# Seven block products in place of eight for six of the 16 row tiles of each FFN gate/up pair

## The chip, the cores and the metric

One core of a Trainium2 chip runs the kernel. The metric is the device time of one execution in microseconds. Three executions of the kernel before are shown; their median is 2152.19 us.

## The reference

An encoder trunk of two layers over 256 tokens of width 2048, in float32. Layer 0 mixes with a Conformer convolution and a windowed attention side by side, layer 1 with a short gated convolution. Behind each stands a SwiGLU FFN with D_FF = 5632, and it is the FFNs that the change touches:

```python
def swiglu_ffn(h, w_gate, w_up, w_down):
    return (jax.nn.silu(h @ w_gate) * (h @ w_up)) @ w_down

# for each layer:
    x = x + mixer(rms_norm(x, mix_norm_g[layer]))
    h = rms_norm(x, ffn_norm_g[layer])
    x = x + swiglu_ffn(h, w_gate[layer], w_up[layer], w_down[layer])
```

## The kernel before

**Numbers and slots.** Every float32 operand is split in two parts, high (rounded to fp32r) and low (the rest), and a product is three matmuls into one PSUM bank: high × high, high × low, low × high (L510 to L512 in `slots`). Activations lie transposed in SBUF, as stationary operands of 128x128: `xT_hi`, `xT_lo` hold the normed input with 16 row tiles of the model width, each for two token halves (t = 0, 1). Weights stream. A slot is 2 row tiles of 512 columns, 512 KB: SP loads it into `w_raw`, ScalarE makes `w_hi` (L871), and the low part `w_lo` is made by VectorE for even slots (L1216) and by GpSimd for odd ones (L464). TensorE then runs 2 row tiles × 2 token halves × 3 = 12 matmuls of 512 columns on it. `w_raw`, `w_hi` and `w_lo` are rings of 4: ScalarE's high of slot s waits until TensorE has used slot s − 4, and SP's load of slot s until the low of slot s − 4 is made.

**Jobs and banks.** A job is a run of slots that ends in one pair of PSUM banks (`pair0`, `pair1`, `pair2`, one bank for each token half). The order of all work is written out by hand, each engine's queue on its own, with the numbers of slots as the common clock: "lows(a, b)" on VectorE stands for the low parts of the slots a to b − 1, "highs(a, b)" for ScalarE's.

**The FFN.** For each of the 11 column blocks of 512 of D_FF: a gate job (16 row tiles, 8 slots, pair 0), an up job (8 slots, pair 1). ScalarE reads the gate pair through SiLU, scaled by the norm's `rstd`, into `gated` (L925); VectorE multiplies the up pair by `rstd` and `gated` into `mixed` (L1271); TensorE transposes `mixed` in 8 small matmuls (L546) in the middle of the next gate job, ScalarE (L892) and VectorE (L1242) split the result into `yT_hi` and `yT_lo`. After all 11 blocks the down projection runs as four jobs, one for each 512 columns of the model width, with 22 slots each over all 44 row tiles of y; VectorE adds each pair into the residual `xs` (L1290, `add_pair`). The blocks 1 to 10 are a hardware loop on each engine; the down jobs are straight code.

**The first block of an FFN** shares its time with the end of the mixer: the last of four blocks of `xs` is transposed and split (`x_split`: L1230, L882, L1235), and the norm is formed (`norm_stats`, `norm_root`), since `rstd` is only needed where the first gate is read. TensorE's `first_block` waits for each x block just ahead of the slots that use it.

## Time and profile before

| | us |
|---|---|
| timed executions, median (lowest, highest) | 2152.19 (2150.77, 2154.49) |
| the profiled execution, from its first to its last instruction | 2149.2 |
| busy: TensorE matmuls, VectorE, ScalarE, GpSimd | 2109.6, 828.8, 994.1, 981.8 |
| GpSimd's low parts (L464), 370 of them | 899.4 |
| VectorE's low parts (L1216), 370 of them | 514.8 |
| ScalarE's high parts (L871), 740 of them | 782.0 |

The page gives no other time of the profiled execution than its span; the median of the timed ones is 3.0 us above that. A matmul's duration in a row (0.39 us) is longer than the distance to the next, since matmuls overlap in the array: their pace is read from the starts. A row of a group gives the smallest, the middle and the largest duration.

### The profile page before, as it was taken

The page shows a single profiled execution, that of the slowest core. Times are in us where ns is not written, and L with a number is a line of the kernel's source. Part 1 is how long each engine was busy: PE and PEld are TensorE (multiplying, and loading weights), DVE is VectorE, ACT ScalarE, POOL GpSimd, SP SyncE. Part 2 cuts the span into 40 slices and gives each one's busy share as a digit, 9 for nine tenths or more (in the row PEclk, how much of TensorE's full clock was granted, in tenths as well). Part 3 has the DMA queues.
Part 4 walks back from the last instruction along what each step waited for, and adds up shares of the span by engine and source line. Part 5 has one row for each costly group of instructions (what it writes and reads, how often), then busy time and mean ns, then how long its engine had stood idle before and what let it go on. Part 6 is the DMA issues. An engine that isn't in the chain of part 4 may idle for free.

```text
span 2149.2 us, 26716 instructions
## 1 busy us (share of the span) xinstructions
PE 2109.6 (98%) x9780; PEld 1757.2 (82%) x9780; DVE 828.8 (39%) x932; ACT 994.1 (46%) x1208; POOL 981.8 (46%) x471
## 2 busy tenths in 40 slices
PE   8999889999999999999999999999999999999999
PEld 6888678888888888888888888888888888888887
DVE  4786854323323322333243444442232232322221
ACT  6677555444444443444444444454444444443332
POOL 3676634444444444444344444444444444444443
PEclk9999999999999999999999999999999999999999
DMA  7543446666666665555566555566666666655554
GB/s 235 167 129 108 147 137 188 184 194 188 187 192 185 186 195 193 186 189 191 181 189 199 183 182 187 193 185 190 194 182 189 193 188 189 191 188 193 192 192 165
DMA packets 208930, 393.65 MB, mean 183 GB/s; under 512 B 12000, under 2 KB 22240, under 8 KB 208864
## 3 DMA queue, kind: packets, MB, share of 16 engines
q1 hardware_dynamic: 208576, 392.22, 58.3%
q8 instruction: 44, 0.72, 0.1%
q10 hardware_dynamic: 288, 0.53, 0.1%
q14 instruction: 22, 0.18, 0.0%
HBM read 390.60 MB, written 2.10 MB: 183 GB/s over the span
## 4 chain that ended last, share of the span: by engine, by line
PE 55%; issue 30%; POOL 9%; DVE 4%; ACT 2%; DMA 1%; POOLq 0%; DVEq 0%; SPq 0%; ACTq 0%
PE pair L510 18%; PE pair L512 18%; PE pair L511 18%; POOL w_lo L464 8%; PE tbank L546 1%; DVE pair L1319 1%; DVE w_lo L1216 1%; ACT w_hi L871 1%; POOL cv L477 1%; DMA w_raw<-in_w_in 1%; PE pair L530 0%; PE pair L531 0%; PE pair L532 0%; DVE xs L1290 0%; ACT products L960 0%
## 5 line engine op out<-in xcount | busy, mean ns | idle before, releaser
L464 POOL TENSOR_TENSOR w_lo<-w_raw,w_hi 128x1024 fp32r<-128x1024 f32 x370 | 899.4, 2431 | 1152.5 <-ACT w_hi L871 1152.5
L871 ACT ACTIVATE w_hi<-w_raw 128x1024 fp32r<-128x1024 f32 x740 | 782.0, 1060 | 932.6 <-PE pair L512 904.4
L1216 DVE TENSOR_TENSOR w_lo<-w_raw,w_hi 128x1024 fp32r<-128x1024 f32 x370 | 514.8, 1393 | 1203.0 <-ACT w_hi L871 1202.8
L510 PE MATMUL pair<-w_hi,xT_hi 128*128 128x512 f32 x1920 | 751.3, 391 | 1.8 <-DVE w_lo L1216 1.0
L512 PE MATMUL pair<-w_hi,xT_lo 128*128 128x512 f32 x1920 | 747.9, 390 | 0.0
L511 PE MATMUL pair<-w_lo,xT_hi 128*128 128x512 f32 x1920 | 747.8, 389 | 0.0
L510 PEld LDWEIGHTS pair<-w_hi,xT_hi 128*128 128x128 f32 x1920 | 360.8, 188 | 77.5 <-POOL w_lo L464 1.7
L512 PEld LDWEIGHTS pair<-w_hi,xT_lo 128*128 128x128 f32 x1920 | 360.7, 188 | 75.3
L511 PEld LDWEIGHTS pair<-w_lo,xT_hi 128*128 128x128 f32 x1920 | 361.0, 188 | 73.9
L510 PE MATMUL pair<-w_hi,yT_hi 128*128 128x512 f32 x704 | 274.3, 390 | 0.0
L512 PE MATMUL pair<-w_hi,yT_lo 128*128 128x512 f32 x704 | 273.9, 389 | 0.0
L511 PE MATMUL pair<-w_lo,yT_hi 128*128 128x512 f32 x704 | 273.9, 389 | 0.0
L512 PEld LDWEIGHTS pair<-w_hi,yT_lo 128*128 128x128 f32 x704 | 132.1, 188 | 27.5
L510 PEld LDWEIGHTS pair<-w_hi,yT_hi 128*128 128x128 f32 x704 | 132.1, 188 | 27.3
L511 PEld LDWEIGHTS pair<-w_lo,yT_hi 128*128 128x128 f32 x704 | 132.2, 188 | 27.2
L477 POOL TENSOR_TENSOR cv<-products,cv 128x256 f32<-128x256 f32 x96 | 83.4, 893 | 2.6
L510 PE MATMUL pair<-w_hi,mT_hi 128*128 128x512 f32 x128 | 52.4, 410 | 10.9 <-DVE mT_lo L1532 9.4
L1319 DVE SCALAR_TENSOR_TENSOR pair<-uT,cols,pair 128x256 f32<-128x256 f32 x139 | 59.2, 479 | 1.1
L925 ACT ACTIVATE gated<-pair,rstd 128x512 f32<-128x512 f32 x54 | 34.2, 686 | 40.6 <-PE pair L512 40.6
L511 PE MATMUL pair<-w_lo,mT_hi 128*128 128x512 f32 x128 | 51.0, 399 | 0.0
L512 PE MATMUL pair<-w_hi,mT_lo 128*128 128x512 f32 x128 | 50.9, 398 | 0.0
L510 PE MATMUL pair<-w_hi,zT_hi 128*128 128x512 f32 x128 | 50.2, 392 | 0.0
(132 smaller groups left out, 1116.4 us busy)
## 6 DMA issues: line engine op xcount, KB each, us to landing
w_raw<-in_w_gate SPq DMA_DIRECT2D x176, 512.0 KB, 4.3
w_raw<-in_w_up SPq DMA_DIRECT2D x176, 512.0 KB, 3.9
w_raw<-in_w_down SPq DMA_DIRECT2D x176, 512.0 KB, 4.2
w_raw<-in_sc_in SPq DMA_DIRECT2D x96, 512.0 KB, 4.4
w_raw<-in_w_in SPq DMA_DIRECT2D x52, 512.0 KB, 3.9
w_raw<-in_w_out SPq DMA_DIRECT2D x32, 512.0 KB, 3.7
w_raw<-in_sc_out SPq DMA_DIRECT2D x32, 512.0 KB, 4.3
xs<-in_x SPq DMA_DIRECT2D x4, 512.0 KB, 8.5
```

Source lines behind the costliest of these rows:

```text
L464: nc.gpsimd.tensor_tensor(w_lo[:, place, :, :], w_raw[:, place, :, :], w_hi[:, place, :, :].bitcast(F32), ALU.subtract).then_inc(w_lo_odd, 1)
L477: nc.gpsimd.tensor_tensor(cv[:, c, :], products[:, n % PRODUCTS, :], cv[:, c, :], ALU.add).then_inc(pool_tap_done, 1)
L510: nc.tensor.matmul(o, hi[:, k, tok(t)], w_hi[:, r, kk, :], start=first, stop=False)
L511: nc.tensor.matmul(o, hi[:, k, tok(t)], w_lo[:, r, kk, :], start=False, stop=False)
L512: mm = nc.tensor.matmul(o, lo[:, k, tok(t)], w_hi[:, r, kk, :], start=False, stop=end)
L546: mm = nc.tensor.transpose(tbank[b][:, n * P:(n + 1) * P], source, ident)
L871: nc.scalar.activation(w_hi[:, r, :, :], w_raw[:, r, :, :], ACT.Copy).then_inc(w_hi_ready, 1)
L925: ins = nc.scalar.activation(dest[:, t, :], pairs[pair][t][:, :], func, scale=rstd[:, t:t + 1])
L1216: nc.vector.tensor_tensor(w_lo[:, r, :, :], w_raw[:, r, :, :], w_hi[:, r, :, :].bitcast(F32), ALU.subtract).then_inc(w_lo_even, 1)
L1319: nc.vector.scalar_tensor_tensor(dest, u, w, acc, ALU.mult, ALU.add).then_inc(tap_done, 1)
```

## The change

**The unit.** Gate and up of one column block no longer are two jobs but one `unit`. Of the 16 row tiles, the tiles 0 to 2 and 4 to 6 are taken as the two blocks of a 2x2x2 block product: the two token halves are the block rows, the two groups of tiles the inner index, gate and up weights the block columns. The eight block products of it are replaced by seven, of sums and differences of activation blocks (`xS_hi`, `xS_lo`, and the place of tiles 0 to 2 of the second half in `xT`) and of weight blocks. VectorE overwrites the four loaded weight blocks (3 row tiles × 512 columns, 768 KB each, in `s_raw`) with differences in four steps (`remake`: place 0 twice, places 2 and 3 once). The other ten row tiles stay ordinary slots of two tiles (`REST_K`). A unit has 17 ring places ("ops"): seven products (ops 0, 1, 3, 5, 6, 9, 12) of 9 matmuls and ten slots of 12.

**Low parts.** In a unit GpSimd makes those of the ops 8, 11 and 14 (`POOL_PLACES`), VectorE all others, the products' too (128x1536). Outside the units they alternate as before.

**Sums.** Products that belong to more than one result are added by VectorE from pair 2 into `snap` in four steps of 512 columns (the first after a copy by ScalarE, `snapshot`), and `gate_sums` and `up_sums` (1024 columns each) add the banks of pair 0 and pair 1. SiLU reads `snap`, `multiply` forms `mixed` from `snap` and `gated`. Up is not scaled by `rstd` there; the down sum into `xs` is (`add_down`).

**Chunks.** SBUF does not hold y for all blocks beside `s_raw`, so the FFN runs in three chunks of 3, 4 and 4 units, each with its share of the down projection (four jobs over 12, 16 and 16 row tiles) and its four sums into `xs`. The last y block of a chunk is used at the end of the first two jobs (`("end", ...)`).

**Around it.** The x sums for the units are made where the blocks 0 and 1 of x are split (`sums_first`, `sums_second`), during the output projection of the mixer. All hardware loops become straight code. `bg` of the gated mixer loads its slots in plain order.

```diff
+SK = 3
+UNIT_OPS = 17
+POOL_PLACES = (8, 11, 14)
+PRODUCT_PLACES = {0: 0, 1: 1, 3: 0, 5: 3, 6: 0, 9: 2, 12: 3}
+MADE = {3: 1, 6: 2, 9: 3, 12: 4}
+REST_K = ((3, 7), (8, 9), (10, 11), (12, 13), (14, 15))
+CHUNKS = ((0, 3), (3, 7), (7, 11))
 RMS_EPS = 1e-6
 LN_EPS = 1e-5
...
+    def unit(self, name):
+        self.units[name] = (len(self.units), self.slots, list(self.pair_uses))
+        for i in range(UNIT_OPS):
+            self.operand(i not in PRODUCT_PLACES, i in POOL_PLACES)
+        self.pair_uses = [uses + 1 for uses in self.pair_uses]
...
+                for ch, (u0, u1) in enumerate(CHUNKS):
+                    for i in range(u0, u1):
+                        n, o, _ = UNIT[(layer, i)]
+                        if n:
+                            sp.wait_ge(t_made, 4 * n)
+                            low_done(sp, UNIT_BASE[n - 1] + 6)
+                        block(0, gates, 0, i)
+                        block(1, ups, 4, i)
+                        rest(o + 2, ups, 0, i)
+                        if n:
+                            low_done(sp, UNIT_BASE[n - 1] + 9)
+                        block(2, ups, 0, i)
+                        rest(o + 4, ups, 1, i)
+                        if n:
+                            low_done(sp, UNIT_BASE[n - 1] + 12)
+                        block(3, gates, 4, i)
+                        rest(o + 7, gates, 0, i)
+                        rest(o + 8, ups, 2, i)
+                        rest(o + 10, gates, 1, i)
+                        rest(o + 11, ups, 3, i)
+                        rest(o + 13, ups, 4, i)
+                        rest(o + 14, gates, 2, i)
+                        rest(o + 15, gates, 3, i)
+                        rest(o + 16, gates, 4, i)
...
+            def unit(layer, i, before=None, norm=None, last_out=None):
+                n, o, uses = UNIT[(layer, i)]
+                a, e = pairs[2][0][:, :], pairs[2][1][:, :]
+                b, a2 = pairs[0][0][:, :], pairs[0][1][:, :]
+                c = pairs[1][0][:, :]
+                if norm is not None:
+                    pe.wait_ge(lo_ready, LOW[("x", norm, 0, 0)] + 1)
+                pe.wait_ge(pair_read[2], uses[2])
+                product(o, a, xT_hi[:, 0:SK, tok(0)], xT_lo[:, 0:SK, tok(0)], True)
+                if norm is not None:
+                    pe.wait_ge(lo_ready, LOW[("s4", norm)] + 1)
+                pe.wait_ge(pair_read[1], uses[1])
+                product(o + 1, c, xS_hi[:, 2, :, :], xS_lo[:, 2, :, :], True, False)
+                rest(o + 2, 0, 1, (False, True))
+                if norm is not None:
+                    read_out(last_out)
+                    x_transposes(norm, NJ - 1)
+                product(o + 3, e, xT_hi[:, 0:SK, tok(1)], xT_lo[:, 0:SK, tok(1)], True)
+                if norm is not None:
+                    x_split(norm, 2)
+                rest(o + 4, 1, 1, (False, False))
+                if before is not None:
+                    y_transposes(layer, before)
+                pe.wait_ge(pair_read[0], uses[0])
+                product(o + 5, b, xT_hi[:, 4:4 + SK, tok(0)], xT_lo[:, 4:4 + SK, tok(0)], True, False)
+                pe.wait_ge(snapped, n + 1)
+                product(o + 6, a, xS_hi[:, 0, :, :], xS_lo[:, 0, :, :], True)
+                rest(o + 7, 0, 0, (False, True))
+                rest(o + 8, 2, 1, (False, False))
+                pe.wait_ge(u2_ready, n + 1)
+                product(o + 9, a, xS_hi[:, 1, :, :], xS_lo[:, 1, :, :], True)
+                rest(o + 10, 1, 0, (False, False))
+                if norm is not None:
+                    x_split(norm, 3)
+                rest(o + 11, 3, 1, (False, False))
+                product(o + 12, a2, xT_hi[:, 4:4 + SK, tok(1)], xT_lo[:, 4:4 + SK, tok(1)], False, False)
+                rest(o + 13, 4, 1, (False, False), (True, True))
+                rest(o + 14, 2, 0, (False, False))
+                rest(o + 15, 3, 0, (False, False))
+                rest(o + 16, 4, 0, (False, False), (True, True))
...
+            def silus(layer, i):
+                n, o, uses = UNIT[(layer, i)]
+                act.wait_ge(pair_read[0], uses[0] + 1)
+                if n:
+                    act.wait_ge(mixed_ready, n)
+                for t in range(TT):
+                    ins = nc.scalar.activation(gated[:, t, :], snap[:, t, :], ACT.Silu, scale=rstd[:, t:t + 1])
+                ins.then_inc(gated_ready, 1)
+            def snapshot(n, o):
+                act.wait_ge(w_used, o + 1)
+                if n:
+                    act.wait_ge(gated_ready, n)
+                nc.scalar.activation(snap[:, 0, :], pairs[2][0][:, :], ACT.Copy).then_inc(snapped, 1)
...
+            def unit(layer, i, at, before=None, norm=None):
+                n, o, _ = UNIT[(layer, i)]
+                highs(at, o + 4)
+                if before is not None:
+                    silus(layer, before)
+                snapshot(n, o)
+                highs(o + 4, o + 7)
+                if norm is not None:
+                    x_highs(norm, NJ - 1)
+                    x_squares(NJ - 1)
+                highs(o + 7, o + 8)
+                if before is not None:
+                    y_highs(layer, before)
+                highs(o + 8, o + 9)
+                if norm is not None:
+                    norm_root(norm)
+                highs(o + 9, o + 10)
+                highs(o + 10, o + 13)
+                highs(o + 13, o + 17)
+                if norm is not None:
+                    act.wait_ge(rstd_ready, norm + 1)
+                return o + 17
...
+            def remake(n, step, dest, a, b):
+                nc.vector.tensor_tensor(s_raw[:, dest, :, :], s_raw[:, a, :, :], s_raw[:, b, :, :],
+                                        ALU.subtract).then_inc(t_made, 1)
+            def bank_sum(dest, bank, source):
+                return nc.vector.tensor_tensor(dest, bank, source, ALU.add)
+            def gate_sums(layer, i):
+                n, o, uses = UNIT[(layer, i)]
+                dve.wait_ge(w_used, o + UNIT_OPS)
+                dve.wait_ge(u3_ready, n + 1)
+                bank_sum(snap[:, 0:2, :], banks[0][:, :, :], snap[:, 0:2, :]).then_inc(pair_read[0], 1)
+            def up_sums(layer, i):
+                n, o, uses = UNIT[(layer, i)]
+                dve.wait_ge(w_used, o + 14)
+                dve.wait_ge(pair_read[2], uses[2] + 1)
+                bank_sum(snap[:, 2:4, :], banks[1][:, :, :], snap[:, 2:4, :]).then_inc(pair_read[1], 1)
+            def multiply(layer, i):
+                n, o, uses = UNIT[(layer, i)]
+                dve.wait_ge(pair_read[1], uses[1] + 1)
+                dve.wait_ge(gated_ready, n + 1)
+                nc.vector.tensor_tensor(mixed[:, :, :], snap[:, 2:4, :], gated[:, :, :],
+                                        ALU.mult).then_inc(mixed_ready, 1)
+            def y_lows(layer, i):
+                k = BK * (i - [u0 for u0, u1 in CHUNKS if u0 <= i][-1])
+                for t in range(TT):
+                    low_of_group(("y", layer, i, t), yT_hi, yT_lo, slice(k, k + BK), t)
+            def unit(layer, i, at, before=None, after=None, norm=None):
+                n, o, uses = UNIT[(layer, i)]
+                lows(at, o + 2)
+                dve.wait_ge(s_loaded[2], 16 * (n + 1))
+                remake(n, 1, 0, 2, 0)
+                lows(o + 2, o + 3)
+                if before is not None:
+                    gate_sums(layer, before)
+                if after is not None:
+                    after()
+                lows(o + 3, o + 4)
+                if before is not None:
+                    multiply(layer, before)
+                else:
+                    lows(o + 4, o + 5)
+                dve.wait_ge(t_made, 4 * n + 1)
+                remake(n, 2, 0, 1, 0)
+                if before is not None:
+                    lows(o + 4, o + 5)
+                lows(o + 5, o + 7)
+                if norm is not None:
+                    x_split(norm, NJ - 1)
+                dve.wait_ge(t_made, 4 * n + 2)
+                remake(n, 3, 2, 1, 2)
+                lows(o + 7, o + 8)
+                if before is not None:
+                    y_lows(layer, before)
+                lows(o + 8, o + 9)
+                if norm is not None:
+                    norm_stats(norm)
+                lows(o + 9, o + 10)
+                remake(n, 4, 3, 3, 0)
+                dve.wait_ge(w_used, o + 7)
+                if n:
+                    dve.wait_ge(gated_ready, n)
+                bank_sum(snap[:, 1, :], pairs[2][0], snap[:, 0, :]).then_inc(u2_ready, 1)
+                lows(o + 10, o + 11)
+                dve.wait_ge(u2_ready, n + 1)
+                if n:
+                    dve.wait_ge(mixed_ready, n)
+                bank_sum(snap[:, 2, :], pairs[2][1], snap[:, 1, :]).then_inc(w_sum_ready, 1)
+                lows(o + 11, o + 13)
+                dve.wait_ge(w_used, o + 10)
+                dve.wait_ge(w_sum_ready, n + 1)
+                bank_sum(snap[:, 1, :], pairs[2][0], snap[:, 1, :]).then_inc(u3_ready, 1)
+                lows(o + 13, o + 14)
+                dve.wait_ge(u3_ready, n + 1)
+                bank_sum(snap[:, 3, :], pairs[2][1], snap[:, 1, :]).then_inc(pair_read[2], 1)
+                lows(o + 14, o + 17)
+                up_sums(layer, i)
+                return o + 17
...
```

## Rows read from the trace of the kernel before

**Rows 1.** Page: busy us (share of span) xinstructions; granted clock in 40 slices.

```profile
PE 2109.6 (98%) x9780; PEld 1757.2 (82%) x9780; DVE 828.8 (39%) x932; ACT 994.1 (46%) x1208; POOL 981.8 (46%) x471
...
PEclk9999999999999999999999999999999999999999
```

**Rows 2.** Waits, whole span: who waited for whom, us, times, longest.

```profile
ACT w_hi L871 <- PE pair L512: 904.4, 595, 2.6
...
PE pair L510 <- DVE mT_lo L1532: 9.4, 1, 9.4
```

**Rows 3.** Timeline, TensorE, in block 9 of FFN 0: start, us, engine, line.

```profile
734.48 0.39 PE L512 MATMUL pair<-w_hi,xT_lo 128*128 128x512 f32 x1
734.71 1.03 PE L546 MATMUL tbank<-tables,mixed 128*128 128x128 f32 x8
...
741.05 0.39 PE L510 MATMUL pair<-w_hi,xT_hi 128*128 128x512 f32 x1
```

**Rows 4.** Timeline, ScalarE, same stretch.

```profile
735.45 1.09 ACT L892 ACTIVATE yT_hi<-tbank 128x512 f32 x2 [2.20 <-PE tbank L546]
...
741.25 1.06 ACT L871 ACTIVATE w_hi<-w_raw 128x1024 fp32r<-128x1024 f32 x1 [1.66 <-PE pair L512]
743.97 1.06 ACT L871 ACTIVATE w_hi<-w_raw 128x1024 fp32r<-128x1024 f32 x1 [1.66 <-PE pair L512]
```

**Rows 5.** Timeline, VectorE, 640 to 800.

```profile
650.77 1.41 DVE L1216 TENSOR_TENSOR w_lo<-w_raw,w_hi 128x1024 fp32r<-128x1024 f32 x1 [2.12 <-ACT w_hi L871]
...
661.65 1.97 DVE L1216 TENSOR_TENSOR w_lo<-w_raw,w_hi 128x1024 fp32r<-128x1024 f32 x1 [4.21 <-ACT w_hi L871]
...
679.60 1.41 DVE L1271 SCALAR_TENSOR_TENSOR mixed<-pair,rstd,gated 128x512 f32<-128x512 f32 x2 [0.40 <-PE pair L512]
...
724.02 1.41 DVE L1271 SCALAR_TENSOR_TENSOR mixed<-pair,rstd,gated 128x512 f32<-128x512 f32 x2 [0.40 <-PE pair L512]
...
736.21 1.29 DVE L1242 TENSOR_TENSOR yT_lo<-tbank,yT_hi 128x512 f32 x2 [1.71 <-ACT yT_hi L892]
```

**Rows 6.** Timeline, TensorE: two stalls, in brackets.

```profile
274.87 0.79 PE L510 MATMUL pair<-w_hi,mT_hi 128*128 128x512 f32 x1 [9.44 <-DVE mT_lo L1532]
...
343.75 0.50 PE L510 MATMUL pair<-w_hi,xT_hi 128*128 128x512 f32 x1 [0.41 <-POOL w_lo L464]
```

**Rows 7.** Windows: us, busy of each engine (xinstructions), clock, DMA share, GB/s.

```profile
10.00:15.00 5.00, 3.68 (x12) 3.06 (x13) 4.26 (x7) 3.73 (x8) 1.54 (x1) 1.00 1.05 388
150.00:164.00 14.00, 12.70 (x97) 12.62 (x96) 9.73 (x13) 9.21 (x17) 10.74 (x10) 0.88 0.45 134
330.00:380.00 50.00, 49.59 (x226) 40.83 (x226) 20.77 (x21) 24.71 (x30) 22.89 (x9) 1.00 0.62 193
820.00:1060.00 240.00, 240.00 (x1077) 199.07 (x1076) 72.27 (x66) 100.60 (x107) 107.69 (x44) 1.00 0.58 190
```

**Rows 8.** Lines L1216, L1235, L1319: duration ns min/median/max, first and last start.

```profile
L1216 DVE TENSOR_TENSOR w_lo<-w_raw,w_hi x370: 1208/1226/3422, 9.3 to 2132.3; 128x1024 fp32r<-128x1024 f32 x185
...
L1235 DVE TENSOR_TENSOR xT_lo<-scaled,xT_hi x32: 679/690/950, 11.9 to 1429.1; 128x512 fp32r<-128x512 f32 x32
...
L1319 DVE SCALAR_TENSOR_TENSOR pair<-uT,cols,pair x139: 471/477/491, 73.3 to 254.3; 128x256 f32<-128x256 f32 x139
```

**Rows 9.** Timeline, GpSimd, 640 to 670.

```profile
648.70 2.40 POOL L464 TENSOR_TENSOR w_lo<-w_raw,w_hi 128x1024 fp32r<-128x1024 f32 x1 [4.56 <-ACT w_hi L871]
...
660.13 2.40 POOL L464 TENSOR_TENSOR w_lo<-w_raw,w_hi 128x1024 fp32r<-128x1024 f32 x1 [4.20 <-ACT w_hi L871]
```

**Rows 10.** Timeline, VectorE, at the first gate block of FFN 0.

```profile
334.77 1.29 DVE L1230 TENSOR_TENSOR scaled<-tbank,cols 128x512 f32<-128x512 f32 x2 [0.79 <-PE tbank L546]
...
340.90 0.16 DVE L1254 SCALAR_TENSOR_TENSOR rstd<-newton,root 128x2 f32<-128x2 f32 x1
```

**Rows 11.** Timeline, ScalarE, same stretch.

```profile
335.50 1.24 ACT L882 ACTIVATE xT_hi<-scaled 128x512 fp32r<-128x512 f32 x2 [2.77 <-DVE scaled L1230]
...
338.77 1.28 ACT L912 ACT_TABLE_LOAD   x1
```

More of the change, by code:

```diff
@@ L70, in job @@
         self.jobs[name] = (self.slots, pair, self.pair_uses[pair])
-        self.slots += k_tiles // slot_k
+        for _ in range(k_tiles // slot_k):
+            self.operand(True, self.slots % 2 == 1)
         self.pair_uses[pair] += 1
@@ new lines, in rest @@
+            def rest(o, q, pair, first, last=(False, False)):
+                r = o % RING
+                low_done(pe, o)
+                for kk in range(SLOT_K):
+                    k = REST_K[q][kk]
+                    for t in range(TT):
+                        b = pairs[pair][t][:, :]
+                        end = last[t] and kk == SLOT_K - 1
+                        nc.tensor.matmul(b, x_hi(k, t), w_hi[:, r, kk, :], start=(first[t] and kk == 0), stop=False)
+                        nc.tensor.matmul(b, x_hi(k, t), w_lo[:, r, kk, :], start=False, stop=False)
+                        mm = nc.tensor.matmul(b, x_lo(k, t), w_hi[:, r, kk, :], start=False, stop=end)
+                mm.then_inc(w_used, 1)
@@ L647, in _ @@
             narrow("kv", 2, SN)
-            slots("q0", 0, 6, xT_hi, xT_lo, last=SD)
+            slots("q0", 0, 6, x_hi, x_lo, last=SD)
             pe.wait_ge(qk_normed, 1)
@@ new lines, in ffn @@
+            def ffn(layer, norm, last_out, norm_after):
+                for ch, (u0, u1) in enumerate(CHUNKS):
+                    if ch == 0:
+                        unit(layer, 0, None, norm, last_out)
+                    else:
+                        unit(layer, u0)
+                    for i in range(u0 + 1, u1):
+                        unit(layer, i, i - 1)
+                    down(layer, ch, norm_after if u1 == NF else None)
+            ffn(0, 1, ("conv_out", NJ - 1), 2)
+            for b in range(2):
+                x_split(2, b)
+                slots(("cg", 0), 2 * b, 2 * b + 2, x_hi, x_lo, last=SD)
@@ L1170, in mixer_block @@
-                act.wait_ge(w_used, s0 + 3 * SD + per * rep)
+                highs(s0 + 2 * SD + 7, s0 + 3 * SD + 3)
+                pair = JOB[("bg", j)][1]
+                act.wait_ge(w_used, s0 + 3 * SD)
                 for t in range(TT):
```

814 lines of the change are left out of this document (514 added, 300 removed).

## The prediction

> **What bounds the kernel now.** I read the busy shares first: TensorE is busy 98% of the span, VectorE 39%, ScalarE and GpSimd 46% each, and TensorE's clock is at its full level (2.4 GHz) in nearly all of it [rows 1]. Then the waits: ScalarE waits 595 times, 904 us in all, for TensorE to release a place of the ring, while TensorE's longest wait for another engine's result is one of 9.4 us, ahead of the FFNs [rows 2]. So the time is the count of matmuls times their spacing. ScalarE's highs, one for each slot of 12 matmuls, start 2.72 us apart (741.25, 743.97): **0.2267 us** a matmul, as the 734.48 to 734.71 of two neighbours also has it [rows 3, 4]. One gate/up pair of blocks is 192 matmuls, 43.53 us; the products `mixed` come 44.42 us apart (679.60, 724.02), so its 8 transposes cost the other 0.90 [rows 3, 5]. The path has no slack there. The clock fell only behind stalls: in 150 to 164 its mean is 0.88; one stall of 0.41 us, at 343.75, left 330 to 380 at 1.00 [rows 6, 7].
>
> **What is removed.** An op is one ring place of the new unit: P for a block product (3 row tiles, one token half, 9 matmuls), R for an ordinary slot (2 row tiles, both halves, 12 matmuls). A unit has 7 P and 10 R: 63 + 120 = 183 matmuls where 192 were, 9 × 0.2267 = 2.04 us less. 22 units: **−44.9 us**. The down projections keep 88 slots per FFN and only change order; the transposes stay. If TensorE never waits, a unit takes 42.39 us.
>
> **What VectorE gets.** Prices with nobody in the way: a low of 128x1024, both inputs in SBUF, 1.226; of 128x512, 0.690; so 128x1536 is an estimate of 1.76 by that slope [rows 8]. Two lows of y, one operand in PSUM, take 1.29 [rows 5]; so 0.69 for one 128x512 bank sum and, an estimate, 1.22 for a double one. Per unit: 7 R lows 8.6; 7 P lows 12.3; 4 remakes of weight differences (128x1536) 7.0; `multiply` 1.2; two lows of y 1.3; four bank sums of 512 2.8, two of 1024 2.4. Sum **35.6 us**, 84% of 42.4, where 8 lows and the two pairs for a block make about 12.5 now. ScalarE: 10 × 1.06, 7 × about 1.5 (1.06 for 1024, 1.24 for two of 512), two pairs of 1.1 to 1.3, a snapshot 0.6: 24 us, loose [rows 4, 11]. GpSimd: 3 × 2.40 = 7.2 us [rows 9].
>
> **The collision.** Here lies the real price. VectorE's low at 661.65 starts while GpSimd's runs from 660.13 to 662.53 and takes 1.97 us: 0.88 of overlap + 1.09. The one at 650.77, overlap 0.33, takes 1.41. Alone it is 1.23 [rows 5, 8, 9]. So the op does not slow down, it waits until GpSimd's whole op has ended. An op with an operand in PSUM never does: 139 conv taps have 471 to 491 ns, though GpSimd works beside them (10.7 of the 14 us of 150 to 164) [rows 7, 8]. The Trainium skill says the same (SBUF — State Buffer, "SBUF: two separate sides"): a VectorE op with two SBUF inputs and a GpSimd op that reads SBUF contend for one port pair, an exclusive lock. By that rule, which speaks against leaving any low on GpSimd, a unit has up to 3 × 2.40 us of VectorE's time more; the rows above agree. Of the 26 VectorE ops of a unit 19 are of the kind that waits. Fully exposed, 7.2 us bring VectorE's load to **42.8 us**, as long as TensorE's. A part of it is not exposed, since VectorE waits there anyway.
>
> **A unit step by step.** Zero is the start of op 0. TensorE's ends are 11.56 for op 4, 12.46 for the transposes behind it, 14.50 op 5, 16.54 op 6, 19.26 op 7, 21.98 op 8, 24.02 op 9. A hop from TensorE to ScalarE costs 0.20 (the next slot's first matmul starts at 741.05, the high at 741.25) [rows 3, 4]; from ScalarE to a low I take 0.05, from a low to TensorE 0.12, estimates between nothing and that 0.20; VectorE's neighbours overlap by 0.08 (two lows of 0.69 in 1.29). From the transposes: y highs 12.66 to 13.75, high 8 to 14.81, GpSimd's low 8 from 14.87 to 17.27. VectorE is done with low 7 at 13.8, does the y lows to 15.1 and is then blocked to 17.27; low 9 to 18.96, remake 4 to 20.64. Product 9 needs the first bank sum, done at 21.24: in time for 21.98. But at 20.64 GpSimd gets the port for low 11, until 23.04, so low 10 is done at 24.19 and op 10 starts at 24.31 instead of 24.02: **0.3 us of stall**. With 0.1 us more for each VectorE op it is 0.75; with every hop 0.1 longer too, about 1.1. Low 14 (28.3 to 30.8) meets a VectorE that has run ahead. Sixteen units have this form: 16 × 0.3 = **4.8 us** (0 to 17.6). The four that begin a later chunk have no y work, but a `down` sum of 1.4 on VectorE; I take 0.5 each, **2 us** (0 to 6).
>
> **The first unit of each FFN** also carries the last x block and the norm. Today these hold VectorE from 334.77 to 341.06 with its waits, and ScalarE from 335.50 through highs and squares to a table load at 338.77; only the 0.41 us of stall at 343.75 comes of it [rows 6, 10, 11]. In the new unit VectorE comes to the x block only at 11.0, behind low 6. ScalarE then has highs and squares until 15.6 ahead of high 7, so low 7 ends at 17.7 where TensorE wants it at 16.54 (1.2 of stall); the root and its steps push low 9 to 22.8 and the sum for product 9 to 25.1 against 23.2 (1.9); GpSimd's low 11 costs another 0.9. That is 4 us each, and where such a stall drops the clock, about 1.7 more (a mean of 0.88 over 14 us is 3.4 us at half speed [rows 7]). I take 5 each, **10 us** (4 to 16).
>
> **At nothing.** The x sums: at most 13 VectorE steps of 0.5 to 0.6 us, some 7 us, ahead of a low that TensorE wants 10.9 us later (cover gone: 3 us, twice). The sums of the chunks' down results into xs, 16 pairs more of 1.4 us, in a stage where VectorE is busy 30% [rows 7]. A chunk's last y block, whose products come behind 4 to 6 slots of 2.72. The loads: up to 2.6 MB are asked for at once, but backlogged queues move 388 GB/s in 10 to 15, and a unit needs 8.4 MB in 42.4 us, 198 GB/s [rows 7]; in SP's queue the block loads stand behind low 11, 13 and 14, some 10 us ahead of their highs. Loops turned into straight code: the down stage is straight already, and TensorE is busy 240 of its 240 us [rows 7].
>
> **Sum.** −44.9 + 4.8 + 2 + 10 = −28.1 on the span of 2149.2: 2121.1. The median of the timed runs, 2152.2, is 3.0 above that span: **2124 us**.
>
> **Rivals.** (A) *All hidden.* The sums come in time, only the first units lose 2 us each: −44.9 + 4 gives 2111 us. For it: my stall of 0.3 us is smaller than the error of the steps. Against: the lock of [rows 5, 9]. Chance 0.25. (B) *Most of the gain is given back.* VectorE's ops and hops cost 0.1 more each: 17.6 + 6 + 14 against 44.9, −7.3: 2145 us. For it: every hop but one is an estimate. Chance 0.15. (C) *VectorE becomes the bound, slower than before.* Its place is from one gate sum to the next: 42.8 us with all blocks exposed, and 26 ops whose waits cost 0.06 us each make 44.4, the point from which it decides. At 0.10 a unit takes 45.4: 1.0 × 22 + 10 is 32 more, 2184 us. For it: the full load is within 1% of TensorE's. Against: two thirds of the block at low 8 fall where VectorE waits anyway, and y's two lows show an overlap, not a gap. Chance 0.07. (D) *The clock.* A stall in each unit drops TensorE to half for 3.4 us, 1.7 lost each: −28 + 22 × 1.7 = +9, 2161 us. Against: 0.41 us did not do it [rows 6, 7]. Chance 0.05.
>
> **How the numbers follow.** Forecast 2124 (its own spread 2114 to 2140) 0.48, A 0.25, B 0.15, C 0.07, D 0.05. The range goes from just below A to beyond B, 2107 to 2150, and leaves out C and D. About 0.2%, 4.3 us, is what a measurement can tell from no change. Faster: 0.48 + 0.25 + 0.11 of B, 0.84; same: 0.04 of B and 0.01 of the slow ones, 0.05; slower 0.11.
>
> **What would show it.** Products `mixed` 42.4 to 43.2 us apart within a chunk (C: above 44.4). TensorE idle ahead of ops 9 and 10, behind VectorE's sum or low 10, and hardly elsewhere. VectorE busy 83 to 98% of the unit stages, its SBUF lows of up to 4 us where GpSimd overlaps, its bank sums never longer. In the first units, idle ahead of ops 7 and 9. A clock below 1 in the unit stages would be D. The forecast is wrong if VectorE is late at the y lows already, if waits in its queue cost over 0.05 each, or if double bank sums are dearer than 1.22.

## The result, and the profile after

The changed kernel takes **2123.2 us** (2120.2 to 2126.2), the kernel before on the same chip 2151.5 (2150.8 to 2154.5): ratio 0.987, 95% interval 0.9855 to 0.9885. Its profiled execution took 2120.17 us, with a span of 2118.4, which is 30.8 less than before.

The page (columns as in [rows 1]), then the share of each engine in the chain that ended last:

```profile
PE 2069.6 (98%) x9582; PEld 1721.4 (81%) x9582; DVE 1302.7 (61%) x1310; ACT 1099.2 (52%) x1260; POOL 740.8 (35%) x361
...
PEclk9999999999999999999999999999999999999999
...
PE 88%; DVE 4%; issue 4%; ACT 2%; POOL 1%; DMA 0%; DVEq 0%; SPq 0%; ACTq 0%; POOLq 0%
```

TensorE has 198 matmuls fewer (22 × 9) and is busy 98% as before; VectorE has gone from 39% to 61%. What TensorE waited for, whole span (us, times, longest). "Answers [rows 2]" means here and below that the same view of the kernel before stands in that group:

```profile
PE pair L636 <- DVE uT_lo L1896: 9.4, 1, 9.4
PE pair L696 <- DVE snap L1922: 7.1, 2, 4.8
```

The first row is the old wait ahead of the FFN. The second is new: two waits of a product for VectorE's bank sum. The products `mixed` of FFN 0, one for each unit, show where those two do not lie (timeline, VectorE; answers [rows 5]):

```profile
569.16 1.22 DVE L1942 TENSOR_TENSOR mixed<-snap,gated 128x1024 f32<-128x1024 f32 x1
...
611.54 1.22 DVE L1942 TENSOR_TENSOR mixed<-snap,gated 128x1024 f32<-128x1024 f32 x1
...
653.91 1.22 DVE L1942 TENSOR_TENSOR mixed<-snap,gated 128x1024 f32<-128x1024 f32 x1
```

They are 42.38 and 42.37 us apart. The prediction gave 42.39 to a TensorE that never waits. So an interior unit has **no stall**, and from 611 to 654 TensorE is busy throughout. All new waits of TensorE lie in the first unit of each FFN. TensorE's stalls in FFN 0's (timeline, idle before in brackets; answers [rows 6]):

```profile
328.46 0.50 PE L711 MATMUL pair<-w_hi,xT_hi 128*128 128x512 f32 x1 [0.42 <-DVE w_lo L1533]
...
343.57 0.50 PE L711 MATMUL pair<-w_hi,xT_hi 128*128 128x512 f32 x1 [2.33 <-DVE w_lo L1533]
...
351.60 0.50 PE L696 MATMUL pair<-w_hi,xS_hi 128*128 128x512 f32 x1 [2.28 <-DVE snap L1922]
...
354.33 0.50 PE L711 MATMUL pair<-w_hi,xT_hi 128*128 128x512 f32 x1 [0.37 <-DVE w_lo L1533]
```

These are ops 2, 7, 9 and 10, 5.4 us in all. FFN 1's has one, at op 9, and the matmuls behind it are 0.43 us apart, not 0.23 (same view):

```profile
1426.06 0.79 PE L696 MATMUL pair<-w_hi,xS_hi 128*128 128x512 f32 x1 [4.78 <-DVE snap L1922]
1426.65 0.63 PE L697 MATMUL pair<-w_lo,xS_hi 128*128 128x512 f32 x1
1427.08 0.63 PE L698 MATMUL pair<-w_hi,xS_lo 128*128 128x512 f32 x1
...
1431.77 0.46 PE L712 MATMUL pair<-w_lo,xT_hi 128*128 128x512 f32 x1
```

The 13 steps from 1426.06 to 1431.77 take 5.71 us where 13 × 0.2267 is 2.95. So FFN 1 loses 4.8 + 2.8 = 7.6 us. The windows say the same (answers [rows 7]): the first units, with an interior stretch between:

```profile
330.00:380.00 50.00, 45.02 (x200) 36.35 (x199) 42.52 (x37) 29.50 (x32) 8.69 (x3) 1.00 0.51 177
611.00:654.00 43.00, 43.00 (x196) 35.69 (x195) 34.97 (x29) 24.26 (x24) 8.15 (x3) 1.00 0.58 203
...
1400.00:1454.00 54.00, 49.22 (x209) 40.09 (x208) 42.48 (x38) 27.96 (x31) 7.32 (x3) 0.94 0.48 166
```

**The account.** −44.9 for the matmuls, + 5.4 + 7.6 = −31.9, where the span shows −30.8. 1.1 us stays unassigned.

One cost of that size lies ahead of the units. From the end of the old 9.4 us wait to the first matmul of the FFN, TensorE takes 49.56 us (273.94 to 323.50), where the kernel before took 48.37 (274.87 to 323.24). The profiled kernels of the next sections that leave this stretch alone take 49.4 to 49.6 each. The matmuls of this output projection come 0.233 us apart, not 0.227, at a granted clock of 1.00 from 289 on in both kernels. The x sums on VectorE, straight code and another place for the stationary operand (`uT` for `mT`) are all new there; no run separates them, so the cause stays open. In this pair of profiles the cost hardly shows in the span, since the old wait ended 0.93 us earlier.

### The profile page after: what moved, and what is told of

It is laid out like the page before. It is cut to its first block, busy times and chain, and to the rows that moved or that the text cites. A ratio compares the mean times of both kernels' runs of the same rounds, so it can differ in the third digit from the quotient of the medians.

```text
span 2118.4 us, 24220 instructions
## 1 busy us (share of the span) xinstructions
PE 2069.6 (98%) x9582; PEld 1721.4 (81%) x9582; DVE 1302.7 (61%) x1310; ACT 1099.2 (52%) x1260; POOL 740.8 (35%) x361
## 4 chain that ended last, share of the span: by engine, by line
PE 88%; DVE 4%; issue 4%; ACT 2%; POOL 1%; DMA 0%; DVEq 0%; SPq 0%; ACTq 0%; POOLq 0%
PE pair L636 14%; PE pair L638 14%; PE pair L637 14%; PE pair L711 9%; PE pair L713 9%; PE pair L712 9%; PE pair L696 5%; PE pair L698 5%; PE pair L697 5%; PE tbank L726 2%; DVE w_lo L1533 1%; ACT w_hi L1110 1%; DVE pair L1683 1%; POOL cv L603 1%; DVE s_raw L1918 0%
## 5 line engine op out<-in xcount | busy, mean ns | idle before, releaser
L591 POOL TENSOR_TENSOR w_lo<-w_raw,w_hi 128x1024 fp32r<-128x1024 f32 x260 | 656.3, 2525 | 1362.6 <-ACT w_hi L1110 1362.6
L711 PE MATMUL pair<-w_hi,xT_hi 128*128 128x512 f32 x880 | 343.5, 390 | 3.1 <-DVE w_lo L1533 3.1
L713 PE MATMUL pair<-w_hi,xT_lo 128*128 128x512 f32 x880 | 342.7, 389 | 0.0
L712 PE MATMUL pair<-w_lo,xT_hi 128*128 128x512 f32 x880 | 342.7, 389 | 0.0
L1533 DVE TENSOR_TENSOR w_lo<-s_raw,w_hi 128x1536 fp32r<-128x1536 f32 x154 | 276.7, 1806 | 97.7 <-ACT w_hi L1110 97.5
L1110 ACT ACTIVATE w_hi<-s_raw 128x1536 fp32r<-128x1536 f32 x154 | 229.2, 1488 | 167.7 <-PE pair L713 120.9
L636 PE MATMUL pair<-w_hi,xT_hi 128*128 128x512 f32 x512 | 201.3, 393 | 1.0 <-DVE w_lo L1533 1.0
L638 PE MATMUL pair<-w_hi,xT_lo 128*128 128x512 f32 x512 | 199.6, 390 | 0.0
L637 PE MATMUL pair<-w_lo,xT_hi 128*128 128x512 f32 x512 | 199.5, 390 | 0.0
L711 PEld LDWEIGHTS pair<-w_hi,xT_hi 128*128 128x128 f32 x880 | 165.4, 188 | 39.6 <-DVE w_lo L1533 5.5
L713 PEld LDWEIGHTS pair<-w_hi,xT_lo 128*128 128x128 f32 x880 | 165.4, 188 | 34.5
L712 PEld LDWEIGHTS pair<-w_lo,xT_hi 128*128 128x128 f32 x880 | 165.5, 188 | 34.4
L1918 DVE TENSOR_TENSOR s_raw<-s_raw 128x1536 f32<-128x1536 f32 x88 | 156.3, 1776 | 0.0
```

Source lines behind the costliest of these rows:

```text
L591: nc.gpsimd.tensor_tensor(w_lo[at], raw(o), w_hi[at].bitcast(F32), ALU.subtract).then_inc(w_lo_pool, 1)
L636: nc.tensor.matmul(o, hi(k, t), w_hi[:, r, kk, :], start=first, stop=False)
L637: nc.tensor.matmul(o, hi(k, t), w_lo[:, r, kk, :], start=False, stop=False)
L638: mm = nc.tensor.matmul(o, lo(k, t), w_hi[:, r, kk, :], start=False, stop=end)
L711: nc.tensor.matmul(b, x_hi(k, t), w_hi[:, r, kk, :], start=(first[t] and kk == 0), stop=False)
L712: nc.tensor.matmul(b, x_hi(k, t), w_lo[:, r, kk, :], start=False, stop=False)
```

## Why no interior stall: who comes to the port first

The prediction had GpSimd's low 11 take the port just ahead of VectorE's low 10, at the price of 0.3 us. Here is the unit whose op 0 starts at 607.92. "Port" is what VectorE's ops with two SBUF inputs and GpSimd's ops wait for each other at (timelines of ScalarE, VectorE, GpSimd):

```profile
620.12 1.09 ACT L1152 ACTIVATE yT_hi<-tbank 128x512 fp32r<-128x512 f32 x2 [2.04 <-PE tbank L726]
...
627.43 1.06 ACT L1110 ACTIVATE w_hi<-w_raw 128x1024 fp32r<-128x1024 f32 x1 [1.66 <-PE pair L713]
...
624.20 2.05 DVE L1533 TENSOR_TENSOR w_lo<-s_raw,w_hi 128x1536 fp32r<-128x1536 f32 x1 [1.29 <-ACT w_hi L1110]
626.17 1.75 DVE L1918 TENSOR_TENSOR s_raw<-s_raw 128x1536 f32<-128x1536 f32 x1
627.84 0.68 DVE L1922 TENSOR_TENSOR snap<-pair,snap 128x512 f32<-128x512 f32 x1
628.44 1.21 DVE L1533 TENSOR_TENSOR w_lo<-w_raw,w_hi 128x1024 fp32r<-128x1024 f32 x1
...
622.24 2.40 POOL L591 TENSOR_TENSOR w_lo<-w_raw,w_hi 128x1024 fp32r<-128x1024 f32 x1 [26.16 <-ACT w_hi L1110]
628.58 3.35 POOL L591 TENSOR_TENSOR w_lo<-w_raw,w_hi 128x1024 fp32r<-128x1024 f32 x1 [3.94 <-ACT w_hi L1110]
```

The y highs start 12.20 us after op 0, behind the first four transposes (12.66 was predicted, behind all eight). So high 8, GpSimd's low 8 (14.32 against 14.87), low 9 and remake 4 all come about half a us sooner. VectorE asks for low 10 at 628.44, GpSimd for low 11 at 628.58, when ScalarE's high 11 is there: VectorE is **0.14 us ahead**, takes 1.21 unhindered, and it is GpSimd that waits (3.35 = 0.95 + 2.40). GpSimd's arrival hangs on TensorE: high 11 waits for op 7 (`<-PE pair L713`), so it ends at 628.49 however early VectorE is. The Trainium skill (SBUF — State Buffer, "SBUF: two separate sides") says that whichever of the two starts first gets the shared pair for the whole instruction. The rows agree.

## Experiments

Executions of one kernel differ by up to 6 us (2120.2 to 2126.2 above), and two medians of the changed kernel by 3.0 (2123.2, 2120.2). Part of that arises in the first 300 us, where none of these kernels differs from the changed one: the first high of a weight block starts anywhere from 313.9 to 319.8. So beside each median stands, from one profile of each kernel, the change against the changed kernel in two stretches: from ScalarE's first high of a weight block (314.35 in the changed kernel) to the first `mixed` of the second mixer (1084.63), and from FFN 1's first such high (1392.18) to the end. The repeat of the changed kernel shows how well they repeat: 0.0 and 0.1 us. The mixer between them takes 307.5 us in every kernel.

| kernel | median us | ratio (95%) | FFN 0 | FFN 1 on |
|---|---|---|---|---|
| changed, again | 2120.2 | 0.986 (0.985 to 0.988) | 0.0 | +0.1 |
| y highs wait for all transposes | 2124.5 | 0.988 (0.987 to 0.990) | +2.2 | +1.1 |
| ten lows on GpSimd | 2182.3 | 1.015 (1.013 to 1.017) | +30.5 | +29.6 |
| all lows on VectorE | 2114.7 | 0.983 (0.982 to 0.985) | −1.8 | −6.2 |
| norm late | 2117.5 | 0.984 (0.982 to 0.986) | −0.2 | −6.2 |
| first unit's low 8 on VectorE | 2114.3 | 0.983 (0.981 to 0.985) | −0.8 | −5.3 |
| first unit's low 11 on VectorE | 2119.0 | 0.984 (0.982 to 0.985) | +1.0 | −3.5 |
| first units eased | 2108.9 | 0.981 (0.979 to 0.982) | −3.8 | −7.9 |
| eased, all on VectorE | 2108.6 | 0.981 (0.979 to 0.982) | −4.1 | −8.1 |
| nine matmuls back | 2162.8 | 1.005 (1.003 to 1.007) | +20.1 | +21.5 |
| two passes | 2023.0 | 0.940 (0.939 to 0.942) | −49.4 | −48.9 |

**The y highs wait for all eight transposes.** It restores the order that the prediction assumed.

```diff
                 k = BK * (i - [u0 for u0, u1 in CHUNKS if u0 <= i][-1])
+                act.wait_ge(t_ready, GROUP[("y", layer, i, TT - 1)][0] + 1)
                 for t in range(TT):
```

> The changed kernel, but ScalarE's first y high waits for all 8 transposes instead of the first 4, as the steps of the prediction had it. It starts the y highs 0.45 us later. Theory (arrival order): in the changed kernel GpSimd's low 11 asks for the port 0.1 us after VectorE has begun low 10; with the later y highs it asks ahead of low 10, gets the port for 2.40 us, and TensorE stalls at op 10: unit period 42.6 to 42.7 instead of 42.37 in the 16 units with y work, 4 to 6 us on the whole, low 10 with 2 us or more instead of 1.21. Rival (slack): 0.45 us disappear in VectorE's waits: period 42.37, no change beyond 1 us.

Measured: `mixed` 42.70 us apart (613.06, 655.76), 0.32 more than the 42.38 of the changed kernel, and now GpSimd has the port first (timelines of VectorE and GpSimd):

```profile
625.73 2.48 DVE L1534 TENSOR_TENSOR w_lo<-s_raw,w_hi 128x1536 fp32r<-128x1536 f32 x1 [1.30 <-ACT w_hi L1110]
...
630.40 3.19 DVE L1534 TENSOR_TENSOR w_lo<-w_raw,w_hi 128x1024 fp32r<-128x1024 f32 x1
...
630.10 2.40 POOL L591 TENSOR_TENSOR w_lo<-w_raw,w_hi 128x1024 fp32r<-128x1024 f32 x1 [3.51 <-ACT w_hi L1110]
```

Low 10 takes 3.19 us, not 1.21, since GpSimd is 0.3 us ahead. In the time of its unit GpSimd's arrival has not moved (op 0 at 609.44 here, so low 11 at 20.66 in both kernels); VectorE's has, from 20.52 to 20.96. The whole predicted chain is there, its 0.3 us too; what failed was the one assumption on the transposes. The sum over both FFNs, 3.3 us, is below the 4 to 6 expected: each has seven such steps of 0.32 and not eight, and in FFN 1 the half clock behind the 4.78 us stall held for 8 matmuls, not 13, which took back 1.1.

**Ten lows on GpSimd.** Is the port a lock that costs the whole op, or could GpSimd take all ordinary lows off VectorE?

```diff
-POOL_PLACES = (8, 11, 14)
+POOL_PLACES = (2, 4, 7, 8, 10, 11, 13, 14, 15, 16)
```

> The changed kernel with all ten ordinary lows of a unit on GpSimd. Theory (the port is held by one of the two for a whole op): 10 x 2.40 of GpSimd and 20.5 us of VectorE's ops with two SBUF inputs cannot overlap, 44.5 us, so a unit takes 44.5 us or more, and the kernel 2165 to 2190 us. Rival (the two only disturb each other at some starts): GpSimd 24.0 and VectorE 27 us both fit in 42.4, period 42.4 to 42.8, the kernel 2120 to 2132 us.

Measured: 44.87 us a unit, slower than before. Its waits and timelines:

```profile
PE pair L696 <- DVE snap L1922: 47.0, 22, 5.2
...
632.39 7.86 DVE L1533 TENSOR_TENSOR w_lo<-s_raw,w_hi 128x1536 fp32r<-128x1536 f32 x2
...
630.70 4.04 POOL L591 TENSOR_TENSOR w_lo<-w_raw,w_hi 128x1024 fp32r<-128x1024 f32 x1 [2.65 <-ACT w_hi L1110]
636.25 2.38 POOL L591 TENSOR_TENSOR w_lo<-w_raw,w_hi 128x1024 fp32r<-128x1024 f32 x1 [1.52 <-ACT w_hi L1110]
```

Two lows of 1.76 take 7.86 together, and GpSimd's 2.40 becomes 4.04: both engines stand still for each other, and the sum for op 9 is late in every one of the 22 units, by 2.1 us on average. The lock stands.

**All lows on VectorE.** The same line as `()`.

> The changed kernel with no low of a unit on GpSimd. VectorE's load becomes 34.0 + 3 x 1.2 = 37.6 us of 42.37. Theory (TensorE bounds the interior, GpSimd's lows 8 and 11 cause most of the stalls of the two first units): interior period 42.37 as now; in the first units no blocked op, stalls 1 to 3 us each instead of 5.4 and 4.8, no half clock: 2112 to 2119 us. Rival (VectorE is short of time there, the port is not what matters): 3.7 us more load make interior stalls of 0.2 or more and first units of 6 us or more: 2124 to 2135 us.

Measured: interior units stay at 42.39 us, so VectorE alone carries a whole unit's lows. FFN 0's first unit stalls 0.42 + 2.35 + 1.43, FFN 1's 1.43 with the clock at its full level behind it. GpSimd's help brings nothing inside and costs 8.0 us in the first units (1.8 + 6.2 in the table). The stall at op 7 of FFN 0 stays, 2.35 for 2.33: GpSimd has no part in that one.

**Norm late.** The squares behind op 12, the root and its steps at the end of the first units.

```diff
                     x_highs(norm, NJ - 1)
-                    x_squares(NJ - 1)
...
-                highs(o + 8, o + 9)
+                highs(o + 8, o + 13)
+                if norm is not None:
+                    x_squares(NJ - 1)
+                highs(o + 13, o + 17)
                 if norm is not None:
                     norm_root(norm)
-                highs(o + 9, o + 10)
-                highs(o + 10, o + 13)
-                highs(o + 13, o + 17)
-                if norm is not None:
...
-                lows(o + 8, o + 9)
-                if norm is not None:
-                    norm_stats(norm)
-                lows(o + 9, o + 10)
+                lows(o + 8, o + 10)
...
                 lows(o + 14, o + 17)
+                if norm is not None:
+                    norm_stats(norm)
```

> The changed kernel, with the squares of the last x block and the forming of rstd moved from ahead of highs 7 and 9 (ScalarE) and low 9 (VectorE) to behind op 12 and behind low 16 in the two first units. Theory (the norm in the middle of the unit makes the stalls at ops 7 and 9): both units stall under 1.5 us each, no half clock, 9 to 12 us less than the changed kernel: 2109 to 2114 us. Rival (the x block itself, or the port, makes them): stalls of 3 us or more stay, 2118 to 2123 us.

Measured 2117.5, where 2109 to 2114 was expected: half a miss. FFN 1 keeps one stall of 1.32, at op 7, where GpSimd's low 8 (1418.16) is 0.33 us ahead of low 7 (1418.49), which takes 3.44. FFN 0 has a longer one of the same kind (timelines of VectorE, GpSimd, TensorE):

```profile
346.78 3.38 DVE L1531 TENSOR_TENSOR w_lo<-w_raw,w_hi 128x1024 fp32r<-128x1024 f32 x1
...
346.44 2.63 POOL L591 TENSOR_TENSOR w_lo<-w_raw,w_hi 128x1024 fp32r<-128x1024 f32 x1 [23.81 <-ACT w_hi L1110]
...
350.22 0.50 PE L711 MATMUL pair<-w_hi,xT_hi 128*128 128x512 f32 x1 [3.81 <-DVE w_lo L1531]
```

With the squares gone, high 8 came sooner, so GpSimd's low 8 was 0.34 us ahead of VectorE's low 7 and op 7 waited 3.81 us; from 351.53 on eight matmuls came 0.43 apart. A shorter queue on ScalarE brought GpSimd to the port ahead of the op that was urgent.

**Low 8, then low 11, of the first units on VectorE.** Which of GpSimd's blocks costs what?

```diff
-    def unit(self, name):
+    def unit(self, name, on_pool=POOL_PLACES):
...
-            self.operand(i not in PRODUCT_PLACES, i in POOL_PLACES)
+            self.operand(i not in PRODUCT_PLACES, i in on_pool)
...
-                plan.unit((layer, i))
+                plan.unit((layer, i), POOL_PLACES if i else (11, 14))
```

and with `(8, 14)` in the last line.

> The changed kernel with op 8's low of the two first units on VectorE instead of GpSimd. Theory: the one-input op of the norm chain that took 2.18 us while GpSimd held the port takes 0.17, but VectorE pays 1.1 us for the low itself; the stall at op 9 in FFN 0 shrinks by about 1 us (2.3 to 1.3); in FFN 1 remake 4 then starts ahead of GpSimd's low 11 and is not blocked, so 4.8 becomes 1 to 2 with no half clock: 2114 to 2118 us. Rival (low 8 has no part in it): stalls as before, 2119 to 2125 us.

> The changed kernel with op 11's low of the two first units on VectorE instead of GpSimd. Theory: remake 4 of FFN 1 takes 1.75 instead of 3.90 us, its stall at op 9 goes from 4.8 to about 2.6, and the stall at op 10 in FFN 0 (0.37) goes; low 8 still blocks the norm chain, so FFN 0's 2.3 at op 9 stays: 2115 to 2119 us, if a stall of 2.6 leaves the clock alone. Rival (low 11 has no part in it): FFN 1 keeps 4 us or more, 2119 to 2125 us.

FFN 1 of the changed kernel shows both (timelines of VectorE and GpSimd):

```profile
1415.40 0.15 DVE L1622 TENSOR_REDUCE meansq<-sumsq 128x2 f32<-128x8 f32 x1
1415.59 2.18 DVE L1623 TENSOR_SCALAR meansq<-meansq 128x2 f32<-128x2 f32 x1
...
1421.51 3.90 DVE L1918 TENSOR_TENSOR s_raw<-s_raw 128x1536 f32<-128x1536 f32 x1
1425.33 0.68 DVE L1922 TENSOR_TENSOR snap<-pair,snap 128x512 f32<-128x512 f32 x1
...
1415.25 2.49 POOL L591 TENSOR_TENSOR w_lo<-w_raw,w_hi 128x1024 fp32r<-128x1024 f32 x1 [26.97 <-ACT w_hi L1110]
1421.35 2.44 POOL L591 TENSOR_TENSOR w_lo<-w_raw,w_hi 128x1024 fp32r<-128x1024 f32 x1 [3.62 <-ACT w_hi L1110]
```

Low 8 blocks a step of the norm on 128x2 elements for 2.18 us; that holds the root back, and by it low 9 and remake 4. Low 11 then is 0.16 us ahead of remake 4, which takes 3.90, not 1.75, and the sum for op 9 is done at 1426.0. In FFN 0 the order is the other way round: remake 4 at 349.19, low 11 at 349.39. That is why FFN 1 stalled 4.78 us at op 9 and FFN 0 2.28.

With low 8 on VectorE the step takes 0.17 and remake 4 is 0.20 us ahead of low 11 (VectorE, then GpSimd):

```profile
1415.56 0.17 DVE L1623 TENSOR_SCALAR meansq<-meansq 128x2 f32<-128x2 f32 x1
...
1419.12 1.75 DVE L1918 TENSOR_TENSOR s_raw<-s_raw 128x1536 f32<-128x1536 f32 x1
...
1419.32 3.81 POOL L591 TENSOR_TENSOR w_lo<-w_raw,w_hi 128x1024 fp32r<-128x1024 f32 x1 [32.18 <-ACT w_hi L1110]
```

FFN 1's stalls are then 1.42 + 0.39 and its clock stays at its full level; FFN 0's at op 9 is 1.40, not 2.28. With low 11 moved and low 8 kept, the norm's step still takes 2.18 and FFN 1 stalls 2.29. FFN 0 keeps its first three stalls (0.42, 2.36, 2.28) and loses the one at op 10, as expected. But the clock did not stay: eight matmuls come 0.43 us apart shortly behind the 2.28 us stall of FFN 0, and eight behind the 2.29 of FFN 1, which cost some 1.6 us each (8 × 0.2). That is why FFN 0 is 1.0 us longer than in the changed kernel, where the same stalls were followed by no half clock, and why the median of 2119.0 lies at the edge of both expectations. In stalls alone, moving low 8 takes 3.8 us away and moving low 11 2.8, so low 8 is the dearer of the two.

**First units eased.** Norm late, the last x block behind low 7 instead of low 6 on VectorE (behind high 7 on ScalarE), and no low on GpSimd in the two first units (the `plan.unit` line as above, with `()`). The second kernel of this kind does the same with `POOL_PLACES = ()`. The cut shows only what is new against norm late.

```diff
-                highs(o + 4, o + 7)
+                highs(o + 4, o + 8)
                 if norm is not None:
                     x_highs(norm, NJ - 1)
...
                 lows(o + 5, o + 7)
-                if norm is not None:
-                    x_split(norm, NJ - 1)
...
                 lows(o + 7, o + 8)
+                if norm is not None:
+                    x_split(norm, NJ - 1)
```

> The changed kernel itself, beside the three others of this chip, as the base of their comparison: 2120 to 2127 us, interior period 42.37, the two first units with the stalls of the first profile (5.4 and 4.8 us, and a half clock behind the longer ones).

> The changed kernel with three edits of the two first units alone: squares and norm behind op 12 and low 16, the last x block behind low 7 instead of low 6, and no low of these two units on GpSimd. Theory (the stalls there come from the norm chain, from the x block ahead of low 7, and from GpSimd taking the port at low 7, remake 4 or low 10): stalls of 0 to 2 us in each first unit, no half clock, 2108 to 2113 us. Rival (the first unit is late for its backlog out of the mixer's end): 3 us or more of stall remain in FFN 0, 2113 us or more.

> The same as e8, and no low of any unit on GpSimd. Theory (TensorE bounds the interior, VectorE has 4 us to spare without GpSimd): period 42.38, the same time as e8 within 1 us. Rival (the three lows on GpSimd relieve VectorE where it counts): interior stalls, 3 us or more above e8.

Measured on one chip: changed 2120.2, eased **2108.9**, eased and all on VectorE 2108.6. FFN 0's stalls are 0.39 + 0.38 + 1.14 (ops 2, 8 and 9), FFN 1 has none. Op 7 no longer waits: the x block was what had held low 7, though its move was not run by itself. 13.0 us of stall and half clock fall to 1.9, and 11.7 are gained from the first block high on. The repeat of the changed kernel shows its stalls to 0.02 us again (0.40, 2.33, 2.28, 0.38; 4.78): the order at the port is set, not chance. The eased kernel beats both, 1.9% below the kernel before. Once the first units leave GpSimd out, the interior blocks on it are worth nothing.

**Nine matmuls back.** Op 0's nine matmuls are issued twice, so that only the count of the matmuls is undone.

```diff
+                low_done(pe, o)
+                for k in range(SK):
+                    r = o % RING
+                    nc.tensor.matmul(a, xT_hi[:, k, tok(0)], w_hi[:, r, k, :], start=(k == 0), stop=False)
+                    nc.tensor.matmul(a, xT_hi[:, k, tok(0)], w_lo[:, r, k, :], start=False, stop=False)
+                    nc.tensor.matmul(a, xT_lo[:, k, tok(0)], w_hi[:, r, k, :], start=False, stop=(k == SK - 1))
                 product(o, a, xT_hi[:, 0:SK, tok(0)], xT_lo[:, 0:SK, tok(0)], True)
```

> The changed kernel with op 0's nine matmuls done twice in each unit (the first nine are overwritten, so they only take TensorE's time): everything of the change but the saved matmuls. Theory (the gain is the matmul count, the rest of the change costs only its stalls in the first units): period 42.38 + 2.04 = 44.4 in the interior; in the first units the longer op 0 hides up to 2 us of stall each, so 2120 + 44.9 - 2 to 5 = 2160 to 2163 us. Rival (chunks, straight code or VectorE's load bring or cost something of their own): off that by over 3 us.

Measured: `mixed` 44.43 us apart, the 44.42 of [rows 5] again, and the total 0.5% above the kernel before (2152.3 on that chip): the rest of the change costs 10.5 us and shows no saving. The matmuls' part of the gain, by the two stretches, is 20.1 + 21.5 = 41.6 us. Of the 44.9 on paper the longer op 0 hides 1.4 us of FFN 0's stalls (1.29 + 2.29 + 0.39 for 5.4), and FFN 1 has ten matmuls at or near half clock and not 13, 0.7 us; 1.2 us stays unassigned.

**Two passes.** In the units the third of three passes (low part of x by high part of the weights) is left out, 61 matmuls of 183, to bring VectorE's own pace to light.

```diff
-                    nc.tensor.matmul(bank, hi[:, k, :], w_lo[:, r, k, :], start=False, stop=False)
-                    mm = nc.tensor.matmul(bank, lo[:, k, :], w_hi[:, r, k, :], start=False,
+                    mm = nc.tensor.matmul(bank, hi[:, k, :], w_lo[:, r, k, :], start=False,
                                           stop=(stop and k == SK - 1))
...
```

> The changed kernel without the low x high matmuls in the units (the third pass of products and slots is left out, so the result is less exact): TensorE needs 122 matmuls and the transposes, 28.6 us a unit, and something else sets the period. It shows how far VectorE is from being the bound. By the durations in the trace, VectorE's ops back to back make 33.4 us and GpSimd's blocks up to 7.2 more: period 37 to 41 us, VectorE over 93% busy, about 2040 to 2095 us. If waits in VectorE's queue had a price of 0.06 us or more each, as the slower rival of the prediction needs, the period would be 42 us or more.

Measured: 37.9 us a unit (`mixed` at 590.93 and 628.78; 36.6 to 39.5 over FFN 0), about the 37 to 41 expected, but a total of 2023, not 2040 to 2095; that total was mis-summed (22 × 4.5 below 2120 is 2021). From 520 to 600:

```profile
520.00:600.00 80.00, 65.78 (x263) 50.56 (x264) 76.06 (x55) 47.01 (x45) 18.27 (x6) 0.94 0.60 210
```

VectorE is busy 76.06 of 80 us, and TensorE's longest waits are for its results: now it is the bound, at 38 us with GpSimd's blocks in it, **4.5 us below** TensorE's 42.4. Rival C had it at the point of taking over.

## Why the prediction was right, and where not

The forecast was 2124 on a median and 2121.1 on the span; measured were 2123.2 and 2118.4. Most of that closeness is deserved, a part is misses that cancel: 6.8 us predicted in the interior units and 0 measured, 10 predicted in the first units and 13.0 measured, and 1.1 unassigned (−6.8 + 3.0 + 1.1 = −2.7, the 2121.1 against 2118.4).

**The matmul term** (−44.9) holds: 42.38 us a unit against 42.39, and 2.05 us more per interior unit with the nine matmuls back.

**VectorE's load** was good. Its prices, from the trace of the changed kernel (ns min/median/max, first and last start; answer [rows 8]):

```profile
L1533 DVE TENSOR_TENSOR w_lo<-s_raw,w_hi x154: 1743/1758/2761, 316.3 to 2007.0; 128x1536 fp32r<-128x1536 f32 x154
...
L1918 DVE TENSOR_TENSOR s_raw<-s_raw x88: 1744/1753/3896, 325.5 to 2001.5; 128x1536 f32<-128x1536 f32 x88
...
L1922 DVE TENSOR_TENSOR snap<-pair,snap x132: 677/681/1225, 350.9 to 2025.9; 128x512 f32<-128x512 f32 x88, 128x1024 f32<-128x1024 f32 x44
```

1.76 for 128x1536 was the estimate, 0.69 and 1.22 for the sums, which never wait, as predicted. The 34.97 us in the 43 us from 611 to 654 answer the 35.6. (The ops that the prediction lists for a unit are 27, not 26; nothing hangs on it.)

**The interior stall** (4.8 us, and 2 for the chunks' first units) is the step that failed: 6.8 predicted, 0 measured, in the four units that begin a later chunk too. Its working is right but for "the y highs come after all eight transposes"; ScalarE starts on the first four. 0.46 us sooner there turned the order at the port around. The trace of before could have told that: its eight transposes run from 734.71 for 1.03 us, to 735.74, and the y highs start at 735.45, before that end [rows 3, 4].

**The first units** (10 us, 5 each; 4 to 16) measured 13.0: 5.4 and 7.6. Op 9 is the right place in both; op 7 waits in FFN 0 alone. The terms were off in two ways.

At op 7 the mechanism is the predicted one (x block and squares ahead of high 7), but 1.2 us in each FFN were 2.3 in FFN 0 and none in FFN 1. GpSimd has no part in it: the stall is 2.35 with all lows on VectorE. What differs is when VectorE comes to the x block, predicted at 11.0 us after op 0. Op 0 starts at 323.50 in FFN 0 and at 1399.03 in FFN 1 (timeline, VectorE, of the x block's first step in each):

```profile
337.32 1.28 DVE L1547 TENSOR_TENSOR scaled<-tbank,cols 128x512 f32<-128x512 f32 x2
...
1409.29 1.28 DVE L1547 TENSOR_TENSOR scaled<-tbank,cols 128x512 f32<-128x512 f32 x2
```

It is 13.8 us behind op 0 in FFN 0 and 10.3 in FFN 1: in FFN 0 VectorE comes out of the mixer later against TensorE (it ends low 1 at 325.60, 2.1 us behind the start of op 0; in FFN 1 at 1397.14, 1.9 ahead of it).

At op 9 the prediction had 1.9 us, and 0.9 at op 10 for GpSimd's low 11; measured were 2.3 and 0.4 in FFN 0, 4.8 and 0 in FFN 1. Without GpSimd op 9 waits 1.43 in both. The rest comes of GpSimd's blocks, which the prediction put only at op 10: low 8 holds up a step of the norm, for which it had reckoned no wait, and low 11 can come before remake 4. The kernels with low 8, with low 11 and with all lows on VectorE show it. The price of a dropped clock, 1.7 us, was 2.8 (13 matmuls), once and not twice.

**Rivals.** A (all hidden) holds for the interior alone; the eased kernel, 2108.9, is nearly its 2111. B did not come about: the ops have their predicted prices, and an interior unit of 42.38 us leaves no room for dearer hops that TensorE would feel. C is refuted by the period of 42.38 and by the two passes; waits of VectorE and GpSimd for each other that do set the period show with ten lows on GpSimd. D happened once in the changed kernel, behind 4.78 us, not in every unit.

**At nothing.** The x sums, chunk sums, y blocks at a chunk's end, loads (768 KB landing in 7.6 to 8.2 us, medians) and straight code put no new wait on TensorE. Not at nothing was the output projection of the first mixer, 1.2 us longer in all, by the pace of its matmuls.

**What would show it.** `mixed` 42.4 apart: yes. Idle ahead of ops 9 and 10: only in the first units. Idle ahead of op 7 there: in FFN 0 alone. VectorE busy 83 to 98%: 81%. Lows up to 4 us: 3.4 the longest, and a remake of 3.90; bank sums never longer: yes.

## What to carry to other kernels

When work is taken off the bounding engine, count its instructions: here 9 × 0.2267 us per unit was the whole gain on paper, and all other work only had to be hidden. Two engines behind a lock are to be judged by who arrives first at each contested op, not by load alone: list both arrival times, and where they are within half a us, take both orders into the range. Before a helper engine is kept, ask whether the helped one has slack: here VectorE had 4.5 us per unit, the help saved no time in any unit, and it could block urgent ops.
